# A two-block transformer kernel: the second block's first norm taken on raw rows, its factors applied at the exits, and low parts of sixteen weight tiles moved to VectorE

## The reference, cut to what matters

```python
h = rmsnorm_2(h_res, g_mix_pre[l])          # x * rsqrt(mean(x*x) + eps) * g
proj = h @ w_in[l]                          # 1024 -> 512 + 3*512 + 2*1024
u_a, c_g, b_g, v_b, gate_logits = jnp.split(proj, splits, axis=-1)
y_a = fourier_mix(u_a) @ w_fourier[l]       # real part of a 2-D DFT, linear in u_a
conv_in = c_g * v_b
y_b = (b_g * centred_dwconv(conv_in, conv_w_mix[l], conv_b_mix[l])) @ w_conv_out[l]
gates = jax.nn.sigmoid((gate_logits + b_gates[l]).reshape(bn, L, N_BRANCHES, D_MODEL))
merged = gates[:, :, 0] * y_a + gates[:, :, 1] * y_b
mix_out = merged @ w_out[l]
```

## Time and profile before

| | |
|---|---|
| median of 3 runs | 997.16 us (997.02 to 997.22) |
| the profiled execution, its own time | 997.04 us |
| its span, first to last instruction | 995.2 us |
| PE busy | 979.8 us (98%) |
| DVE, ACT, POOL busy | 603.6, 537.0, 294.2 us |
| granted TensorE clock, mean | 0.998 |

### The profile page before, as it was taken

One profiled execution on the slowest core, in us unless ns is written; L12 is line 12 of the kernel. 1 busy time (PEld: TensorE's weight loads), 2 busy tenths in 40 slices (PEclk: granted clock), 3 DMA queues, 4 the chain that ended last, 5 costly groups with the idle time before them and its releaser, 6 DMA issues.

```text
span 995.2 us, 15058 instructions
## 1 busy us (share of the span) xinstructions
PE 979.8 (98%) x6330; PEld 885.4 (89%) x6330; DVE 603.6 (61%) x798; ACT 537.0 (54%) x776; POOL 294.2 (30%) x92
## 2 busy tenths in 40 slices
PE   9999999999999999999999999999999999999997
PEld 7888889999888788889999888799999999999885
DVE  4997946788412554556788222445218589888643
ACT  6676346545333577746554433645453687665532
POOL 0021045566655000025565656455540000000000
PEclk9999999999999999999999999999999999999999
DMA  8553224554655453344545555354444426554531
GB/s 334 173 190 146 85 91 165 186 195 170 211 175 206 170 181 115 127 166 158 188 170 188 193 195 185 140 187 152 173 167 170 169 95 223 183 199 170 198 141 42
DMA packets 24807, 168.51 MB, mean 169 GB/s; under 512 B 2781, under 2 KB 3092, under 8 KB 4900
## 3 DMA queue, kind: packets, MB, share of 16 engines
q1 hardware_dynamic: 24452, 167.22, 47.3%
q10 hardware_dynamic: 288, 0.33, 0.1%
HBM read 166.49 MB, written 1.05 MB: 168 GB/s over the span
## 4 chain that ended last, share of the span: by engine, by line
PE 90%; ACT 4%; DVE 3%; issue 1%; DMA 1%; SPq 0%; DVEq 0%; ACTq 0%
PE bank L642 28%; PE bank L644 27%; PE bank L643 27%; PE bank L842 2%; ACT whi L1143 2%; DVE wlo L1711 1%; DMA raw<-w_stream 1%; PE bank L670 1%; PE bank L810 0%; PE bank L859 0%; PE bank L1051 0%; PE bank L952 0%; PE bank L1035 0%; PE bank L878 0%; PE bank L942 0%
## 5 line engine op out<-in xcount | busy, mean ns | idle before, releaser
L1711 DVE TENSOR_TENSOR wlo<-raw,whi 128x1024 fp32r<-128x1024 f32 (+2 forms) x152 | 263.6, 1734 | 293.9 <-ACT whi L1143 293.8
L2353 POOL TENSOR_TENSOR wlo<-raw,whi 128x1024 fp32r<-128x1024 f32 (+1 forms) x85 | 293.0, 3448 | 435.1 <-ACT whi L1143 427.8
L1143 ACT ACTIVATE whi<-raw 128x2048 fp32r<-128x2048 f32 (+1 forms) x154 | 292.8, 1902 | 147.6 <-PE bank L644 145.4
L642 PE MATMUL bank<-nhi,whi 128*128 128x256 f32 (+3 forms) x832 | 238.2, 286 | 1.2 <-DVE nlo L1719 1.2
L643 PE MATMUL bank<-nlo,whi 128*128 128x256 f32 (+3 forms) x832 | 235.5, 283 | 0.0
L644 PE MATMUL bank<-nhi,wlo 128*128 128x256 f32 (+3 forms) x832 | 235.1, 283 | 0.0
L642 PEld LDWEIGHTS bank<-nhi,whi 128*128 128x128 f32 (+1 forms) x832 | 158.2, 190 | 4.8 <-issue 4.7
L643 PEld LDWEIGHTS bank<-nlo,whi 128*128 128x128 f32 (+1 forms) x832 | 158.3, 190 | 0.1
L644 PEld LDWEIGHTS bank<-nhi,wlo 128*128 128x128 f32 (+1 forms) x832 | 158.3, 190 | 0.0
L642 PE MATMUL bank<-mhi,whi 128*128 128x258 f32 x384 | 109.3, 285 | 1.7 <-DVE mlo L2187 1.0
L644 PE MATMUL bank<-mhi,wlo 128*128 128x258 f32 x384 | 108.4, 282 | 0.0
(11 more groups left out here) (292 smaller groups left out, 1570.9 us busy)
## 6 DMA issues: line engine op xcount, KB each, us to landing
raw<-w_stream SPq DMA_DIRECT2D x154, 1024.0 KB, 4.8
cst<-consts SPq DMA_DIRECT2D x1, 1200.0 KB, 11.6
h<-x_rows SPq DMA_DIRECT2D x4, 256.0 KB, 5.4
raw<-w_stream SPq DMA_DIRECT2D x2, 512.0 KB, 6.6
out_rows<-e SPq DMA_DIRECT2D x4, 256.0 KB, 2.0
e<-g_post SPq DMA_DIRECT2D x1, 512.0 KB, 4.0
raw<-w_stream SPq DMA_DIRECT2D x1, 352.0 KB, 9.6
b<-consts_x SPq DMA_DIRECT2D x1, 272.0 KB
```

What stands on the lines that cost most here:

```text
L642: pe.matmul(out, lhsT.hi, rhs.hi, start=start, stop=False)
L1143: act.activation(whi[j][:, 0:n], raw[j][:, 0:n], ACT.Copy).then_inc(s_hi.up(i))
L1711: dve.tensor_tensor(wlo[j][:, 0:m], raw[j][:, 0:m], whi[j][:, 0:m].bitcast(F32), ALU.subtract).then_inc(s_lod.up(i))
L2353: pool.tensor_tensor(wlo[j][:, m:n], raw[j][:, m:n], whi[j][:, m:n].bitcast(F32), ALU.subtract).then_inc(s_lop.up(i))
```

## The change

The second block's norm goes the way of the other three: `h` is transposed raw in two halves (`half_turn(4, c)`), the gain goes into `nhi`/`nlo`, and the factor of a row is applied where the products leave PSUM. For that the inverse root (one value a row) and its square are put on diagonals by VectorE (`DG4`) and spread over all partitions by two float32 matmuls (`rowf4`); ScalarE copies them to `RSB2` and `RS2`. VectorE multiplies `u` and the gates by the first, `cg` by the second (which covers `cv` as well), `bg` by the first. The same four transposed banks serve for `HT`; the eight separate transposes of `xn` and of `h` go. ScalarE no longer copies `u` and `cg`; the sigmoid reads SBUF after VectorE. Low parts of tiles 101 to 116 are made by VectorE alone. The table of the sigmoid is loaded in front of `hi(101)` and not in front of the gates. `lo(120)` stands behind the last `mlo` of the `ya`/`yb` stage, and `hi(127)`/`lo(127)` stand ahead of the MLP's loop.

```diff
@@ def cut(i):
-    return n if i < OUT_AB + 2 or C0 - 1 <= i < OUT_C + 4 or i >= FOURIER + 2 else n // 2
+    return n if i < OUT_AB + 2 or C0 - 1 <= i < OUT_C + 4 or i >= IN2 + 2 else n // 2
@@ tensor_program
-            for q in range(4):
-                u = begin("res", q)
...
-                        x = pe.transpose(u.t[:, kk * 256 + tt * P:kk * 256 + tt * P + P], h[:, tt, (2 * q + kk) * P:(2 * q + kk + 1) * P], ident)
-            us = [begin("nT", q) for q in range(4)]
...
-                        x = pe.transpose(u.t[:, kk * 256 + tt * P:kk * 256 + tt * P + P],
-                                         xn[:, tt, (2 * q + kk) * P:(2 * q + kk + 1) * P], ident)
+            out_tok(3, DOWN[1], 16, ..., (0, 2, 1, 3),
+                    lambda: half_turn(4, 0))
...
+            us = [begin("u", m) for m in range(2)]
+            for n in range(4):
+                m = n % 2
+                for k in range(n // 2 * 4, n // 2 * 4 + 4):
+                    on.wait_ge(*n_ready(4, k))
+                    x = mm3(us[m].t[:, 0:L2], w[:, k, m * P:m * P + P], nT2[:, k, :], k == 0, k == 7)
+                if n == 0:
+                    half_turn(4, 1)
+            feat(weights(IN2 + 1, 8), IN2 + 1, begin("u", 2), 0, 0, lambda k: n_ready(4, k))
+            u = begin("rowf4")
+            on.wait_ge(*s_dg4.at(1))
+            for j in range(2):
+                x = pe.matmul(u.t[:, j * 256:j * 256 + 256], ones, DG4[:, j * 256:j * 256 + 256], start=True, stop=True)
+            feat(weights(IN2 + 1, 8), IN2 + 1, begin("u", 3), P, 0, lambda k: n_ready(4, k))
@@ scalar_program
+            for c in range(2):
+                half_turn(4, c)
+            row_stats(4)
+            for q in range(4):
...
+                act.activation(HT[:, 2 * q:2 * q + 2, META:L2], ...)
+            tables("sigmoid_and_others")
+            hi(IN2 + 2)
+            act.activation(RSB2[:, META:L2], u.t[:, 0:256], ACT.Copy)
+            act.activation(RS2[:, 2:N2], u.t[:, 256:512], ACT.Copy).then_inc(u.free)
+            hi(IN2 + 3)
...
+            hi(IN2 + 4)
+            hi(IN2 + 5)
@@ the gates
-                act.activation(GT[:, g, :], u.t[:, 0:N2], ACT.Sigmoid, bias=vcol("b_gates", g)).then_inc(u.free)
+                on.wait_ge(*use["gt", g].gone())
+                act.activation(GT[:, g, :], GT[:, g, :], ACT.Sigmoid, bias=vcol("b_gates", g)).then_inc(s_gate.up(g))
@@ ahead of the MLP's loop
+            hi(UP2 + 4)
@@ vector_program
-                dve.tensor_scalar(xn[:, tt, :], h[:, tt, :], small[:, 2 + tt:3 + tt], None, ALU.mult).then_inc(s_xnt.up(tt))
+            half_turn(4, 1)
+            dve.memset(RSB2[:, 0:META], 1.0)
+            dve.memset(RS2[:, 0:2], 1.0).then_inc(s_one.up(0))
+            for j in range(2):
+                on.wait_ge(*s_stat.at(4, 1 + j))
+                for tt in range(2):
+                    x = dve.tensor_scalar(DG4[...], ident, stats[4][2 + j][:, tt:tt + 1], None, ALU.mult)
+            def scaled(dst, u, r):
+                on.wait_ge(*use["rowf4",].gone())
+                on.wait_ge(*u.done())
+                dve.tensor_tensor(dst, u.t[:, 0:r.shape[1]], r, ALU.mult).then_inc(u.free)
+            lo(IN2 + 2)
+            for m in range(3):
+                scaled(UT[:, m, :], use["u", m], RSB2)
+            lo(IN2 + 3)
+            scaled(UT[:, 3, :], use["u", 3], RSB2)
...
+            for m in range(4):
+                if m % 2 == 0:
+                    lo(IN2 + 4 + m // 2)
+                scaled(CG[:, m, :], use["cg", m], RS2)
@@ times bg, in pairs
+                lo(IN2 + 8 + j)
+                for m in (2 * j, 2 * j + 1):
+                    dve.tensor_tensor(CV[:, m, :], CV[:, m, :], u.t[:, 0:N2], ALU.mult).then_inc(u.free)
+                    dve.tensor_tensor(CV[:, m, :], CV[:, m, :], RSB2[:, X0:L2], ALU.mult).then_inc(s_bgr.up(m))
@@ the gates
+                scaled(GT[:, g, :], use["gt", g], RSB2[:, X0:L2])
@@ ya and yb
-                lo(FOURIER + 2 * part + 3)
+                if part == 0:
+                    lo(FOURIER + 3)
...
             merged_lo(7)
+            lo(FOURIER + 5)
@@ ahead of the MLP's loop
+            lo(UP2 + 4)
```

More of the change, by code:

```diff
@@ L355, in plan_banks @@
     banks.take("metaT")
-    out(3, DOWN[1], 16)
-    for q in range(4):
[L358 to L363, removed]
+    out(3, DOWN[1], 16, (), 4)
+    for m in range(2):
+        banks.take("u", m, hold=True)
+    banks.take("tr", 4, 2)
+    banks.take("tr", 4, 3)
+    for m in range(2):
+        banks.drop("u", m)
+    banks.take("u", 2)
+    banks.take("rowf4")
+    banks.take("u", 3)
+    for i in range(2):
+        last[IN2 + i] = (("u", 2 * i + 1), 0)
     banks.take("resm")
@@ L448, in block_kernel @@
         small = sb("small", 256)
-        rows = sb("rows", 32)
+        rows = sb("rows", 40)
         room = place[0]
@@ L486, in block_kernel @@
         GAIN = ["g_mix0", "g_ffn0", "g_mix1", "g_ffn1", "g_mix_pre"]
-        stats = [[rows[:, 8 * t + 2 * i:8 * t + 2 * i + 2] for i in range(4)] for t in range(4)]
+        stats = [[rows[:, 8 * t + 2 * i:8 * t + 2 * i + 2] for i in range(4)] for t in range(5)]
         A = Area("a")
@@ L610, in block_kernel @@
         s_mr, s_mn, s_mhi, s_mlo = (sig(n, [0]) for n in ("mr", "mn", "mhi", "mlo"))
-        s_nrs, s_xnt = sig("nrs", range(2)), sig("xnt", range(2))
+        s_bgr, s_dg4, s_one, s_nodd, s_gate = sig("bgr", range(4)), sig("dg4", range(2)), sig("one", [0]), sig("nodd", range(4)), sig("gate", range(16))
         s_cvid, s_ybhi, s_yblo, s_fthi = (sig(n, range(4)) for n in ("cvid", "ybhi", "yblo", "fthi"))
@@ L622, in n_ready @@
         def n_ready(t, k):
-            return (use["tr", t, k // 2] if t < 4 else use["nT", k // 2]).gone() if k % 2 else s_nlo.at(t, k // 2)
+            if k % 2 == 0:
+                return s_nlo.at(t, k // 2)
+            return use["tr", t, k // 2].gone() if t < 4 else s_nodd.at(k // 2)
         def h_ready(t):
@@ L977, in tensor_program @@
             x.then_inc(u.full)
-            out_tok(3, DOWN[1], 16, lambda k: FF[1][:, k, :], lambda k: [s_fflo.at(1, k // 2)], None, (0, 2, 1, 3))
-            for q in range(4):
-                u = begin("res", q)
[L984 to L987, removed]
-                        x = pe.transpose(u.t[:, kk * 256 + tt * P:kk * 256 + tt * P + P], h[:, tt, (2 * q + kk) * P:(2 * q + kk + 1) * P], ident)
-                x.then_inc(u.full)
-            us = [begin("nT", q) for q in range(4)]
[L991 to L994, removed]
-                        x = pe.transpose(u.t[:, kk * 256 + tt * P:kk * 256 + tt * P + P],
-                                         xn[:, tt, (2 * q + kk) * P:(2 * q + kk + 1) * P], ident)
-                    if tt == 1:
-                        x.then_inc(u.full)
+            out_tok(3, DOWN[1], 16, lambda k: FF[1][:, k, :], lambda k: [s_fflo.at(1, k // 2)], None, (0, 2, 1, 3),
+                    lambda: half_turn(4, 0))
             def blocks(name, tile, n, c0, after=None):
@@ L1006, in tensor_program @@
             on.wait_ge(*s_mlo.at(0))
-            blocks("u", IN2, 4, 0)
+            us = [begin("u", m) for m in range(2)]
+            w = weights(IN2, 8)
+            weights_in(IN2)
+            for n in range(4):
[3 more added lines that the diff above has]
+                    x = mm3(us[m].t[:, 0:L2], w[:, k, m * P:m * P + P], nT2[:, k, :], k == 0, k == 7)
+                if n >= 2:
+                    x.then_inc(us[m].full)
+                if n == 0:
+                    half_turn(4, 1)
+            feat(weights(IN2 + 1, 8), IN2 + 1, begin("u", 2), 0, 0, lambda k: n_ready(4, k))
+            u = begin("rowf4")
+            on.wait_ge(*TC)
+            on.wait_ge(*s_dg4.at(1))
+            for j in range(2):
+                x = pe.matmul(u.t[:, j * 256:j * 256 + 256], ones, DG4[:, j * 256:j * 256 + 256], start=True, stop=True)
+            x.then_inc(u.full)
+            feat(weights(IN2 + 1, 8), IN2 + 1, begin("u", 3), P, 0, lambda k: n_ready(4, k))
             u = begin("resm")
@@ L1150, in evac_turn @@
                     k = 2 * q + kk
-                    act.activation(dst[:, k, c0:c0 + S].hi, u.t[:, kk * 256:kk * 256 + 256], ACT.Copy,
+                    act.activation(dst[:, k, :].hi, u.t[:, kk * 256:kk * 256 + 256], ACT.Copy,
                                    scale=vcol(GAIN[t], k)).then_inc(s_nhi.up(t, k))
@@ L1515, in scalar_program @@
                 hi(DOWN[1] + it + 2)
[L1519 to L1524, removed]
+            for c in range(2):
+                half_turn(4, c)
+            row_stats(4)
             for q in range(4):
[L1526 to L1529, removed]
+                u = use["tr", 4, q]
+                on.wait_ge(*s_nodd.at(q))
                 act.activation(HT[:, 2 * q:2 * q + 2, META:L2], u.t[:, :].rearrange("p (k t) -> p k t", k=2), ACT.Copy).then_inc(u.free)
[L1532 to L1537, removed]
+            tables("sigmoid_and_others")
+            hi(IN2 + 2)
+            u = use["rowf4",]
```

(34 more changed lines are left out.)

36 lines of the change are left out of this document (18 added, 18 removed).

## The result

The changed kernel takes 995.27 us (median of 18 runs, 995.02 to 995.83) against 997.08 (18 runs): ratio 0.9982, 95% interval 0.9975 to 0.9988. That is 1.8 us faster where 4.6 were forecast, and it lies above the range, which ended at 994.6.

The account below looks back on a forecast made before the run. TensorE, busy 98% of the span, was taken as the bound, so only its work and pauses counted. Terms -3.0 (norm), +0.3, -1.2 and -0.7 summed to -4.6 us: 997.04 to 992.4, range 991.2 to 994.6.

Parts of the forecast that it names:

- last bank to first `u` matmul: Second block's norm: `u` starts at 633.52, 5.21 us earlier, priced from the norm inside the first block.
- `u` to the first `cg`: Work added behind the start of `u`: `half_turn(4, 1)` with pauses at `nlo` +1.12 us, `rowf4` +1.07.
- first `dp`: ScalarE and VectorE chain from the end of `cg`, 33.0 us against TensorE's 32.7: +0.3, bounds 0 and +0.8.
- the `mo` stage (lo(120)): Moving `lo(120)` behind the last `mlo` removes 1.36 us of pauses, tile 120 costs 0.2: -1.2, bounds -1.5 and -0.6.
- tile 127: Splitting this tile ahead of the MLP's loop removes TensorE's pause before it: -0.7 us, bounds 0 and -0.75.
- the 0.2 for tile 120: Last sums before the MLP: its low part ready at 771.5, wanted at 771.4; 0.2 us allowed as cost.
- rival A: The chain to tile 101 is late, 1.5 to 3 us longer, pausing TensorE 1 to 2: 993.3 to 994.4; chance 0.14.
- the margin of 0.6: After the second block's norm, tile 101's low part is ready at 648.0 and TensorE wants it at 648.6.
- Rivals B: The two moved tiles, 120 and 127, give nothing, both late: only -2.7 us, 994.3; chance 0.10.
- C: Gates become bound by the line ScalarE, VectorE, ScalarE: slower (1000 at 16 us a pair) 0.05, about equal 0.05.

Follow-up runs that it names:

- e1: Changed kernel with the fifth norm's statistics in a free part of `small`, `rows` back at 32 columns, so nothing behind it moves: 991.83 us, ratio 0.9945.
- e2: Kernel before with `rows` of 40 columns instead of 32 and nothing else changed: 1000.78 us, ratio 1.0038.
- e5: Changed kernel without the memory shift, low parts of tiles 101 to 116 shared with GpSimd again: 992.85 us, ratio 0.9957.
- e6: Changed kernel without the memory shift, splits of tiles 120 and 127 back in their old places: 994.02 us, ratio 0.9968.
- e11: Changed kernel without the memory shift, the sigmoid's table loaded in front of the gates as before: 994.15 us, ratio 0.9970.
- e9: Changed kernel without the memory shift, down-projection operands at distances 512, 768, 256, then everything in SBUF 64 bytes higher: 988.68 us, ratio 0.9916.

## Why the prediction was wrong

**The step that failed** is in the first paragraph: "an edit is worth only the TensorE work that it adds or removes and the pauses in front of TensorE that it opens or closes." There is a third way: it can change the pace of matmuls that it doesn't touch, by moving their operands. The sum has no term for it. Its size, +3.4 to +3.7 us, is shown from both sides: e1 takes it out of the changed kernel (995.27 to 991.83), e2 puts it into the one before (997.06 to 1000.78). With it the forecast of 992.4 would have been 995.8 to 996.1. The case wasn't among the rivals, and the range, made of rivals about waits, couldn't hold it.

**The other terms**, from distances between starts in the two traces, which the shift ahead doesn't touch:

| term | forecast | measured |
|---|---|---|
| last bank to first `u` matmul | -5.21 | 7.87 to 2.60: -5.27 |
| `u` to the first `cg` | +2.19 | 12.87 to 14.62: +1.75 |
| first `dp` | +0.3 | 695.28 to 695.75, less 0.12: +0.35 |
| the `mo` stage (lo(120)) | -1.2 | 24.51 to 23.07: -1.44 |
| tile 127 | -0.7 | 1.39 to 0.48: -0.91 |

Their sum is -5.5 against -4.6; e1's 5.2 in the time of the whole kernel agrees. The price read from the norm inside the first block was right to 0.1 us. The `u` term was 0.4 too dear, in two halves: `rowf4` with its changes of kind took 0.86 of the 1.07 charged (646.64 to 647.75 us, less two steps of 0.126), and `half_turn(4, 1)` with the pauses at `nlo` 0.90 of 1.12 (the first 48 matmuls take 7.02 after and 6.13 before). Of the 0.2 for tile 120 under 0.1 came: its low part ends at 771.49, and it is wanted at 765.81 + 5.76 = 771.57.

**Two slips in the working.** The terms of the chain to the first `dp` add up to 33.2 and not 33.0, which makes +0.5 of the +0.3; measured were +0.35, so that the smaller number fits better by luck. And in rival A a chain 3 us longer, less the margin of 0.6, is a pause of 2.4 and a time of 994.8, beyond the range. Neither bears on the miss.

**Tile 101.** The timelines of ScalarE and VectorE after:

```profile
645.51 1.28 ACT L1141 ACT_TABLE_LOAD   x1
646.81 1.91 ACT L1153 ACTIVATE whi<-raw 128x2048 fp32r<-128x2048 f32 x1
```

```profile
648.75 2.29 DVE L1712 TENSOR_TENSOR wlo<-raw,whi 128x2048 fp32r<-128x2048 f32 x1 [4.38 <-ACT whi L1153]
```

Ready at 651.04, used at 651.34: margin 0.3 instead of 0.6, so rival A came close and didn't happen. The split starts 1.30 us after the table load. The Trainium skill (ScalarE: Activation LUTs, What ACT_TABLE_LOAD costs) adds a drain of about 1380 ns; it doesn't show here either. By the page's figure, an estimate, TensorE would have waited about 1.1 us.

**VectorE alone.** e5 shows its worth, about 1.0 us, most of it through tile 101, which GpSimd would have delivered late. The additions take 292 to 303 ns now, against up to 2494 before and 2145 in e5. To them the 0.2 at the first `dp` can be put at most; it wasn't separated from the later start of the stage.

**Rivals B and C** didn't happen. The gates stay bound by TensorE: it doesn't wait in them again after the first `dp`. e6 shows that the two moved tiles give 2.2 us, the whole of their pauses. The table ahead of tile 101 matters for the opposite end of its stretch: left where it was, it would have cost 1.4 us at the first `dp` (e11), and in front of tile 101 the margin just covered it.

## What to carry to other kernels

Read a diff for what it moves in memory too: one array of 32 bytes more, in front of the operands of a busy matmul, took back 3.4 of 5.2 us without a single wait in the trace. Where the stages outside the edit might have changed, compare how many matmuls start per stretch of equal length; waits and busy shares show nothing. In this kernel the operands of matmuls of 512 columns were best placed at distances that are multiples of 256 bytes. Where an array in front of them must grow, growing it by such a step would keep the distance modulo 256; no run tried that.

## What the runs showed of the hardware that I had not expected

The pace of these matmuls of 512 columns (fp32r, 128 x 128 stationary operands, granted clock 1.00 in the stretches shown) depends on the distance in SBUF of the stationary operand from the weight slots, which hold the moving one, modulo 256 bytes:

| distance mod 256 | distances mod 1024 that were run (first half of the rows) | ns per matmul |
|---|---|---|
| 0 | 256, 512, 768 | 226.7 |
| 192 | 704, 192 | 228.9 |
| 128 | 384, 128 | 232.3 to 232.4 |
| 64, 160, 224 | 832 and 64, 416, 736 | 233.3 |

The distances are worked out from the sizes of the arrays, the paces from the starts of successive matmuls in each trace. The spread, 3%, was there for 1,032 matmuls of this kernel. For 192 the step of 256 is untested, since its two runs cover the same two distances. e9 speaks against the absolute place. The slots were never moved alone, so that it is the moving operand, and not another array that kept its place with them, is the likely reading and not shown. Why it is so (for instance that the two reads meet in the same part of the memory) was only supposed and not tried.

No such cost shows in matmuls with fewer columns whose stationary operand is the weight tile: in the second block the moving operand of those with 258 columns lies 56 + 64 k bytes (modulo 256) from the slots, k being the number of the block of 128 features, and from 651.60 to 687.91 us of the kernel before they start 119.8 ns apart, while those with 256 columns at distance 0 take 120.0. The same operands at other distances weren't tried.
